# Activation operands in flat buffers: other byte addresses for the streamed operands of the matmuls

## What is computed

```python
fx = _swiglu(_pre(hx, norm_w[i, 0], mx[:, 0], mx[:, 1]), ffn_w_gate[i, 0], ffn_w_up[i, 0], ffn_w_down[i, 0])
fc = _swiglu(_pre(hc, norm_w[i, 0], mc[0], mc[1]), ffn_w_gate[i, 0], ffn_w_up[i, 0], ffn_w_down[i, 0])
hx = hx + 0.5 * mx[:, 2] * fx
...
def _swiglu(h, w_gate, w_up, w_down):
    return (jax.nn.silu(h @ w_gate) * (h @ w_up)) @ w_down
```

## Time and profile before

| | us |
|---|---|
| median of 3 runs | 2853.32 (2852.08 to 2854.17) |
| the profiled execution | 2851.07 |
| its span, first to last instruction | 2849.3 |
| PE busy in it | 2770.8 (97%) |
| DVE, ACT, POOL busy | 1770.9, 1204.0, 200.2 |

### The profile page before, as it was taken

The page is one execution under the profiler, slowest core; times in us unless marked ns, Lnnn a source line. Parts: engine busy times, 40 slices in busy tenths (PEclk is TensorE's granted clock), DMA queues, the critical chain, the costliest instruction groups (busy, mean ns, idle before and its releaser), DMA issues.

```text
span 2849.3 us, 45845 instructions
## 1 busy us (share of the span) xinstructions
PE 2770.8 (97%) x17468; PEld 2439.7 (86%) x17468; DVE 1770.9 (62%) x2690; ACT 1204.0 (42%) x1808; POOL 200.2 (7%) x246
## 2 busy tenths in 40 slices
PE   7999999999999999999998999999989999999998
PEld 5888876678888788888876999999879999998998
DVE  5977244847874287732538655667666666667665
ACT  4222223833222243222326555654445555544553
POOL 0100011010100100001100101001000000000001
PEclk9999999999999999999999999999989999999999
DMA  8666222025663346533330556656425666653554
GB/s 305 208 197 184 91 87 89 1 74 177 207 191 117 113 155 192 176 96 97 98 99 19 166 182 187 183 176 212 120 88 177 181 186 186 183 169 98 173 177 137
DMA packets 118688, 424.31 MB, mean 149 GB/s; under 512 B 13280, under 2 KB 14321, under 8 KB 117409
## 3 DMA queue, kind: packets, MB, share of 16 engines
q1 hardware_dynamic: 98528, 353.41, 40.4%
q0 software_dynamic: 18992, 68.09, 8.1%
q10 hardware_dynamic: 1040, 1.05, 0.1%
HBM read 421.45 MB, written 1.05 MB: 148 GB/s over the span
## 4 chain that ended last, share of the span: by engine, by line
PE 88%; DVE 7%; ACT 2%; issue 2%; DMA 1%; SPq 0%; DVEq 0%; ACTq 0%
PE bank L721 28%; PE bank L723 28%; PE bank L722 28%; DVE WL L1559 1%; ACT WH L1222 1%; DMA f_nat<-in_ada_n 1%; DVE rstd L1755 1%; DVE g_max L1857 1%; DVE d_small L1919 1%; PE bank L854 1%; PE bank L962 0%; PE bank L939 0%; DVE g_p L1877 0%; DVE tn L1765 0%; DVE d_p L1928 0%
## 5 line engine op out<-in xcount | busy, mean ns | idle before, releaser
L721 PE MATMUL bank<-XH,WH 128*128 128x256 f32 (+1 forms) x3776 | 1227.1, 325 | 21.6 <-DVE XL L1774 6.2
L722 PE MATMUL bank<-XL,WH 128*128 128x256 f32 (+1 forms) x3776 | 1215.1, 322 | 0.0
L723 PE MATMUL bank<-XH,WL 128*128 128x256 f32 (+1 forms) x3776 | 1214.9, 322 | 0.0
L1559 DVE TENSOR_TENSOR WL<-raw,WH 128x1024 fp32r<-128x1024 f32 (+1 forms) x664 | 806.1, 1218 | 643.3 <-ACT WH L1222 640.1
L1222 ACT ACTIVATE WH<-raw 128x1024 fp32r<-128x1024 f32 (+1 forms) x664 | 681.9, 1034 | 817.4 <-PE bank L723 805.1
L721 PEld LDWEIGHTS bank<-XH,WH 128*128 128x128 f32 x3776 | 723.1, 192 | 83.8 <-issue 11.8
L722 PEld LDWEIGHTS bank<-XL,WH 128*128 128x128 f32 x3776 | 723.5, 192 | 55.1 <-issue 3.1
L723 PEld LDWEIGHTS bank<-XH,WL 128*128 128x128 f32 x3776 | 723.0, 191 | 52.3
L721 PE MATMUL bank<-HH,WH 128*128 128x256 f32 (+1 forms) x1408 | 451.0, 320 | 0.0
L722 PE MATMUL bank<-HL,WH 128*128 128x256 f32 (+1 forms) x1408 | 450.9, 320 | 0.0
L723 PE MATMUL bank<-HH,WL 128*128 128x256 f32 (+1 forms) x1408 | 450.9, 320 | 0.0
(11 more groups left out here) (318 smaller groups left out, 1617.4 us busy)
## 6 DMA issues: line engine op xcount, KB each, us to landing
a_rows<-in_ada_t POOLq DMA_DIRECT2D x124, 512.0 KB, 4.2
raw<-in_ffn_w_gate SPq DMA_DIRECT2D x88, 512.0 KB, 3.6
raw<-in_ffn_w_up SPq DMA_DIRECT2D x88, 512.0 KB, 4.3
raw<-in_ffn_w_down SPq DMA_DIRECT2D x64, 512.0 KB, 3.6
raw<-in_ffn_pre_w_gate SPq DMA_DIRECT2D x44, 512.0 KB, 3.6
raw<-in_ffn_pre_w_up SPq DMA_DIRECT2D x44, 512.0 KB, 4.3
raw<-in_ffn_post_w_gate SPq DMA_DIRECT2D x44, 512.0 KB, 3.6
raw<-in_ffn_post_w_up SPq DMA_DIRECT2D x44, 512.0 KB, 4.3
```

What stands on the lines that cost most here:

```text
L721: nc.tensor.matmul(o, WH[:, j % 4, k, :], high, start=start, stop=False)
L722: nc.tensor.matmul(o, WH[:, j % 4, k, :], low, start=False, stop=False)
L723: return nc.tensor.matmul(o, WL[:, j % 4, k, :], high, start=False, stop=stop)
L1559: nc.vector.tensor_tensor(WL[:, b, 0:d, :], raw[:, b, 0:d, :], WH[:, b, 0:d, :].bitcast(F32), ALU.subtract).then_inc(split_done, 1)
```

## The change

XH and XL become two views of one flat buffer `x_all`, HH and HL two of `h_all`, each with some elements of slack. A view starts at an element offset, chosen for each stage by a table: 0 or 112 for X, 0 or 368 for H. The low view lies 16384 bytes (X) or 45056 bytes (H) behind the high one, as before. `skew` grows by 64 bytes. A norm on 256 columns now always writes columns 256 to 511 of its view, and the product behind it reads them there. No instruction, semaphore or transfer is added or taken away.

```diff
-        XH = sb("XH", [P, DT, 2 * S], F32R)
-        XL = sb("XL", [P, DT, 2 * S], F32R)
+        X_PAD, H_PAD = 128, 368
+        x_all = sb("x_all", [P, 2 * DT * 2 * S + X_PAD], F32R)
...
-        skew = sb("skew", [P, 32])
+        skew = sb("skew", [P, 48])
+
+        def x_view(at, low):
+
+            at += DT * 2 * S if low else 0
+            return x_all[:, at:at + DT * 2 * S].rearrange("p (k n) -> p k n", k=DT)
+
+        NORM_X = (0, 0, 0, 0, 0, 112, 112, 112, 112, 112, 112, 112, 0)
+        MIX_X = (0, 112, 112, 112)
+        FFN_H = (0, 0, 0, 368, 368, 368, 368, 368)
+        x_high = lambda at: x_view(at, False)
+        x_low = lambda at: x_view(at, True)
...
-        HH, HL = arena(("HH", [P, FT, 2 * S], F32R), ("HL", [P, FT, 2 * S], F32R))
+        (h_all,) = arena(("h_all", [P, 2 * FT * 2 * S + H_PAD], F32R))
+
+        def h_view(at, low):
+
+            at += FT * 2 * S if low else 0
+            return h_all[:, at:at + FT * 2 * S].rearrange("p (k n) -> p k n", k=FT)
...
+            n["x"] = NORM_X[n["i"]]
+            n["c0"] = S if t == S else 0
...
+            h_at = FFN_H[hid0 // FT]
...
-                add(Gemm("up", iters, DT, t, src, x_scaled if n["defer"] else x_in, ready, hid0=hid0, i0=i0, ada=tile,
-                         scale=n if n["defer"] else None))
+                add(Gemm("up", iters, DT, t, src, (x_scaled if n["c0"] else x_in)(n["x"]), ready, hid0=hid0, i0=i0, ada=tile,
+                         scale=n if n["defer"] else None)).h_at = h_at
...
-        def out_proj(w, t, ready, gate):
+        def out_proj(w, t, m, gate):
             return add(Gemm("res", 2, DT, t, lambda i, _, b: at(w, i * 4 + b),
-                            x_in, ready, gate=gate))
+                            x_in(MIX_X[m]), mix_ready[m], gate=gate))
```

More of the change, by code:

```diff
@@ L351, in ffn @@
             add(Gemm("res", 2, FT, t, lambda i, _, b: at(f"{wd}{b % 3}", i * 4 + b // 3),
-                     hid_in, lambda k: (hid_low, hid0 + k + 3), gate=gate, scale=n if n["defer"] else None))
+                     hid_in(h_at), lambda k: (hid_low, hid0 + k + 3), gate=gate, scale=n if n["defer"] else None))
             state["hid"] += FT
@@ L1102, in gla_low @@
                 for k in range(DT):
-                    nc.tensor.matmul(bank[4][:, 0:S], a_wh[:, k, :], XH[:, k, S:2 * S], start=(k == 0), stop=False)
-                    nc.tensor.matmul(bank[4][:, 0:S], a_wh[:, k, :], XL[:, k, S:2 * S], start=False, stop=False)
-                    last = nc.tensor.matmul(bank[4][:, 0:S], a_wl[:, k, :], XH[:, k, S:2 * S], start=False, stop=(k == DT - 1))
+                    nc.tensor.matmul(bank[4][:, 0:S], a_wh[:, k, :], x_high(MIX_X[3])[:, k, S:2 * S], start=(k == 0), stop=False)
+                    nc.tensor.matmul(bank[4][:, 0:S], a_wh[:, k, :], x_low(MIX_X[3])[:, k, S:2 * S], start=False, stop=False)
+                    last = nc.tensor.matmul(bank[4][:, 0:S], a_wl[:, k, :], x_high(MIX_X[3])[:, k, S:2 * S], start=False, stop=(k == DT - 1))
                 last.then_inc(gs["low"], 1)
@@ L1711, in scaled_low @@
                 dve.wait_ge(n_high, n["h0"] + k + 1)
[L1712 to L1713 removed]
+                nc.vector.scalar_tensor_tensor(out=x_low(n["x"])[:, k, S:2 * S], in0=xT[:, k, 0:S], scalar=n["weight"](k, 0),
+                                               in1=x_high(n["x"])[:, k, S:2 * S].bitcast(F32), op0=ALU.mult, op1=ALU.subtract).then_inc(n_low, 1)
             def restate(d):
@@ L1773, in rest @@
                             cs = slice(half * S, half * S + S)
+                            xs = slice(n["c0"] + half * S, n["c0"] + half * S + S)
                             last = nc.vector.scalar_tensor_tensor(
-                                out=XL[:, k, cs], in0=tn[:, k % 2, cs], scalar=n["shift"](k, half),
-                                in1=XH[:, k, cs].bitcast(F32), op0=ALU.add, op1=ALU.subtract)
+                                out=x_low(n["x"])[:, k, xs], in0=tn[:, k % 2, cs], scalar=n["shift"](k, half),
+                                in1=x_high(n["x"])[:, k, xs].bitcast(F32), op0=ALU.add, op1=ALU.subtract)
                     else:
-                        last = nc.vector.tensor_tensor(XL[:, k, 0:t], tn[:, k % 2, 0:t], XH[:, k, 0:t].bitcast(F32), ALU.subtract)
+                        last = nc.vector.tensor_tensor(x_low(n["x"])[:, k, 0:t], tn[:, k % 2, 0:t], x_high(n["x"])[:, k, 0:t].bitcast(F32), ALU.subtract)
                     last.then_inc(n_low, 1)
```

54 lines of the change are left out of this document (26 added, 28 removed).

## The result

The changed kernel takes 2824.34 us (median of 4 runs, 2822.68 to 2830.05) against 2853.25 us of the kernel before beside it (2852.08 to 2854.17): ratio 0.9902, 95% interval 0.9885 to 0.9920. So it is faster by 28.9 us, where 53.7 were forecast, and the time lies 12 us above the range. Two things are to be explained: the shortfall, and the spread. The runs of the changed kernel lie 7.4 us apart, those of the kernel before beside them 2.1. Four runs are few, though: in the later measurements twelve runs of the kernel before lie up to 7.3 us apart (2848.38 to 2855.67).

What follows compares the result with a forecast made beforehand. TensorE bounds the kernel, busy 97% of the span. 10.1 (downs) + 35.4 (ups) + 6 (input projections) + 3.2 (output projections) - 1 (waits) = 53.7 us off 2853.3, said as 2799.5; range 2791 to 2812 us, chance 0.85.

Steps and rivals of the forecast that it cites:

- 512-column downs: Down products of the three 512-column FFNs: H comes to remainder 0 and takes X's pace, 1584 matmuls, 10.1 us saved.
- 256-column ups: Up products of the five 256-column FFNs: X at remainder 448 takes H's pace, 5280 matmuls x 6.7 ns, 35.4 us saved.
- "Untouched" 256-column downs: Down products of the 256-column FFNs: 2640 H matmuls stay at remainder 448, so no change in time.
- Input projections: Projections of the retention/dilated and GLA mixers: 1248 matmuls at remainder 448, 6 us taken of at most 8.4.
- a gap that ends with another engine's work: In the mixers' input projections: such gaps don't shrink when TensorE arrives earlier, so 6 of 8.4 us, ends 2 and 8.4.
- Output projections: Output projections of mixers 1, 2 and 3: 480 of 576 matmuls gain H's pace, 3.2 us saved, ends 0 and 3.9.
- The GLA product: Small GLA product, lines 1103 to 1105: 24 matmuls go from distance 32 to 416, within 24 x 7 ns, nothing.
- Transposes of line 962: 192 of some 380 transposes touched by ident and sq moving 64 bytes: 2 us either way for all, kept for the range.
- It isn't the address: Rival: the buffers, not the distance between operand and weights, make the difference; time stays at 2853 us; chance 0.05.
- The supply gives the gain back: Rival: weight transfers beside 256-column ups can't pass 190 GB/s, losing 11 us; about 2816 us; chance 0.06.
- 448 is bad for X: Rival: 256-column X matmuls at remainder 448 pay 6.4 ns each, 45 us more; 2889 us; chance 0.04.

Runs made afterwards that it cites:

- e1: Changed kernel with X at offset 0 everywhere, so only H of the three 512-column FFNs goes to remainder 0; 2843.0 us, ratio 0.9964.
- e4: Kernel of bare matmuls only, sixteen distances between stream and weights in 32-byte steps; at 256 columns, distance 448 ran at 113.3 or 117.7 ns per matmul.
- e5: Bare-matmul kernel with distances 0 to 252 bytes in 4-byte steps, 256 columns; 113.3 ns in all six blocks only at 112 and 192.
- e6: Bare-matmul kernel with distances of high view, low view and a WL shift chosen apart, plus eight row mixtures; two settings at 113.3 ns in all six blocks.
- e12: Bare-matmul scan in 32-byte steps, repeated without an edit; distances 192 and 448 at 113.3 ns in all 18 blocks.
- e7: Changed kernel with both offsets at 28 elements, X and H of the 256-column stages 112 bytes from the weights; 2804.25 us, ratio 0.9830.
- e8: Changed kernel with X of the 256-column stages at 21 elements (84 bytes from the weights) and H at 28; 2859.66 us, ratio 1.0027.
- e9: Bare-matmul kernel with sixty pauses for each of six settings (448, 192, 112, 368, two variants of 192); 0 of 122 blocks at 448 or 192 slow.
- e13: Bare-matmul kernel with sixty pauses and the same six settings, run again unaltered; 14 of 122 blocks at 448 or 192 at 117.8 ns.
- e10: Bare-matmul kernel with sixty pauses at distances 192, 448, 704, 960 and 624, buffer 512 bytes lower; no slow block.
- e11: Changed kernel with the offsets at 48 elements, X and H of the 256-column stages 192 bytes from the weights; 2826.80 us, ratio 0.9902.
- e3: Changed kernel unaltered, profiled and timed again; 2818.20 us, ratio 0.9885.

## Why the prediction was wrong in size, step by step

- *512-column downs, 10.1 us.* Right: 10.5 in their windows, alone (e1) and in the sum.
- *256-column ups, 35.4 us. The step that failed.* It took "5280 matmuls x 6.7", with H's 113.3 ns as the pace of the address. The address has two lasting paces, 113.3 and 117.7. All that had a record in the trace of before was H, and each of its five downs follows an up at 120 ns without a pause. Entered from 120 ns without a pause, the fast pace came every time here: five downs before, five in e1, and six blocks of e4, e5, e6 and e12. The ten downs are what counts in this, as bare blocks are seldom slow behind a pause either. An up has other entries: pauses, sums of squares and the loop's start, and behind these either pace can come (12 of the 20 FFNs in the four profiles at 448 or 192 were slow). Which of these entries decides isn't shown. The ups gave 21.8. With every FFN fast, as distance 112 makes them, they gave 33.3, and the whole kernel took 2801.7 to 2809.6 us, inside the range. The distance as the cause and the 6.7 ns were right; that the address has a second lasting pace was left out of the term.
- *"Untouched" 256-column downs, 0 us.* Wrong by 7.2, for the same reason: a down takes over the pace of its up. It has the same distance as before and was costed as if that settled it. Three slow FFNs, ups and downs together, are 3 x 7.0 = 21.0 us of the 26.8 missing.
- *Input projections, 6 of 8.4 us.* 2.7 came. In mixer 2, 4.1 (119.5 to 115.4), in mixer 3 -1.3. The way out that was named, a gap that ends with another engine's work, is there: TensorE waits there for a_la and a_wl for 2.7 and 1.2 us in place of 2.2 and 0.8:

```profile
PE bank L1141 <- DVE a_la L2034: 2.7, 1, 2.7
PE bank L1123 <- DVE a_wl L2018: 1.2, 1, 1.2
```

  A second one was not: the clock. The windows of the changed kernel around the end of the gap on a_la, and then the two windows around the same gap in the kernel before:

```profile
2533.00:2538.00 5.00, 2.29 (x20) 2.10 (x19) 4.31 (x6) 2.67 (x3) 0.00 (x0) 1.00 0.42 107
2538.00:2543.00 5.00, 5.00 (x32) 5.00 (x31) 0.99 (x1) 0.00 (x0) 0.00 (x0) 0.66 0.65 211
```

```profile
2554.10:2559.10 5.00, 2.78 (x24) 2.57 (x23) 5.00 (x6) 1.82 (x2) 0.00 (x0) 1.00 0.48 135
2559.10:2564.10 5.00, 5.00 (x45) 5.00 (x44) 0.72 (x3) 1.24 (x2) 0.00 (x0) 1.00 0.57 183
```

  Behind the gap 45 matmuls fitted into 5 us before, and 32 after: with 0.66 as its mean clock TensorE has the 1.2 GHz level for two thirds of the window. In the changed kernel (1 - clock) x length comes to 3.4 us in this stretch, in that of before to nothing. It isn't the address: e1, with its ups and projections at distance 0 and the waits of before (2.2 and 0.8), has a drop of 1.7 us there too and takes 86.5 us, 1.7 more than before. All seven other profiles of a whole kernel have at least one drop there; that of before has none. Whether it was spared by chance, one profile of it can't tell.
- *Output projections, 3.2 us.* Nothing in the sum. That of mixer 1 ran at the slow pace (192 x 117.7 ns = 22.6 us of the 22.7), and with distance 112 it gains 1.5 us (23.3 to 21.8). Of these 1.3 are its 192 x 6.7 ns; before, the stretch had a clock of 0.98. Those of mixers 2 and 3 stand behind VectorE in every version, 30.0 to 30.7 us. TensorE waited in them for 4.9 and 3.9 us before and for 5.5 and 5.0 after: what closer matmuls could gain went into longer waits. And the earlier trace rows already had a granted clock of 0.84 and 0.89 there.
- *The GLA product, "nothing".* Right: its 22 steps take 2.58 us after, 2.57 before. *Transposes of line 962, within 2 us.* Right: 287 ns of mean against 288.
- *Rivals.* "It isn't the address" is refuted by e7 and e8, which differ in nothing but 28 bytes in the place of X and lie 55 us apart. "The supply gives the gain back" predicted 2816, the closest number, and is wrong all the same: the second up streams at 192 GB/s, and e7's ups without a wait at the start run at 119.7, 121.6 and 120.8 with TensorE busy throughout, so a piece has its weights in time. "448 is bad for X" didn't hold: even the slow pace there is 2.3 ns better than 120.

Take the forecast's pace for all five FFNs and the profiled executions give its number: 2814.5 with two FFNs at 117.7 ns, less 2 x 7.0, is 2800.5 (an estimate, for a profile in which the clock took only 19.6 us). The forecast is the best case of the change and not its usual one; no profile at 448 had all five fast.

Open: what picks the pace at a pause. It isn't fixed by the length of the pause (e4 against e12, e9 against e13), nor by the program. The multiple of 256 in the distance doesn't exclude the slow pace: by 2048 it came at 192 and 448 (e4) and at 704 and 960 (e13). e10, without any slow block, tells nothing on this. It differs between executions, with 3 of 5 FFNs slow in two profiles, 2 and 4 in one each, but in bare matmuls only 0 to 4 of 18 and 0 to 14 of 122 blocks. Transfers beside the matmuls could be the difference; that wasn't tried. How the two reads meet inside the chip is not told by these runs either. That distances 112 and 368 are free of the slow pace rests on 311 blocks (189 and 122), and for the kernel on one profile with X and H at 112, and H alone in that of e8; its five runs, 7.9 us apart, leave room for a rare slow FFN.

## What to carry to other kernels

Where TensorE is busy without a gap and matmuls of one shape have different mean durations, compare the addresses of stream and weights before anything else; a scan of bare matmuls over the distance, 4 bytes at a time over 256, takes one run, and for the two distances tried with one pace it foretold the stage within 0.1 us in 120 to 130. Look in it for a distance whose pace is the same behind every pause, over repeated executions, and not only for the lowest number: here 112 and 192 tie at 113.3 in the scan, and in the kernel the difference between them is 22.6 us (e7 against e11). A pace read from one stage is good for another only if both are entered in the same way.

## What the runs showed of the hardware that was not expected

- The pace of back-to-back matmuls at the 2.4 GHz level depends on the distance between streamed operand and weights, with a period of 256 bytes and 4 bytes are enough to change it: 113.3 to 123.3 ns at 256 columns (130.0 in single blocks), 226.7 to 234.2 at 512, with the order of the distances not the same for both.
- At the same addresses two paces can each hold for more than a thousand matmuls: 113.3 and 117.8 ns at distance 192. All 20 downs at 448 or 192 behind an up at the same distance had the pace in which the up ended; the second up of the changed kernel took over the slow pace and left it 14 us later.
- A kernel bound by TensorE can thereby have a spread of its own: the eight runs of the changed program (result and e3) lie between 2814.54 and 2830.05 us, while all 33 runs of the kernel before lie between 2848.38 and 2855.67.
- The granted clock falls to the 1.2 GHz level here and there in the mixers, where TensorE has gaps, and not in the same places in each execution. By (1 - clock) x length this came to 19.6 to 31.6 us in eight profiles of the same instruction stream, 23.6 in that of before: another spread, of the size of the terms of the forecast's sum.
- Distance 112 needs up to about twelve matmuls behind a pause to settle at 113.3, and then stays.
